# Own-token experts chosen first, and their u rows dotted during retrieval and gate building, in a conv/DeltaNet/PEER block

## What is computed

```python
def peer(h, w_q, sub_keys, u_tab, v_tab):
    q = (h @ w_q).reshape(B, T, PEER_HEADS, 2, PEER_HALF)        # 8 heads, 2 halves of 128
    s = jnp.einsum('bthpd,hpnd->bthpn', q, sub_keys)             # 128 keys per half
    v1, i1 = lax.top_k(s[..., 0, :], K)                          # K = 16
    v2, i2 = lax.top_k(s[..., 1, :], K)
    cand = (v1[..., :, None] + v2[..., None, :]).reshape(B, T, PEER_HEADS, K * K)
    cidx = (i1[..., :, None] * PEER_NKEYS + i2[..., None, :]).reshape(B, T, PEER_HEADS, K * K)
    top_s, pos = lax.top_k(cand, K)
    eidx = jnp.take_along_axis(cidx, pos, axis=-1)
    gates = jax.nn.softmax(top_s, axis=-1)
    ...  # per token, its 8 * 16 = 128 experts
        act = jax.nn.gelu(jnp.einsum('btd,bted->bte', hb, jnp.take(u_tab, ib, axis=0)))
        return jnp.einsum('bte,bted->btd', gb * act, jnp.take(v_tab, ib, axis=0))
```

## Time and profile before

| | us |
|---|---|
| median of 3 runs | 2196.34 |
| the profiled execution, its own time | 2198.44 |
| its span, first to last instruction | 2196.6 |
| TensorE busy in the span | 1880.5 |
| VectorE busy | 1477.7 |
| ScalarE busy | 729.6 |
| GpSimd busy | 709.8 |

### The profile page before, as it was taken

One profiled execution on the slowest core, in us unless ns is written; L12 is line 12 of the kernel. 1 busy time (PEld: TensorE's weight loads), 2 busy tenths in 40 slices (PEclk: granted clock), 3 DMA queues, 4 the chain that ended last, 5 costly groups with the idle time before them and its releaser, 6 DMA issues. The chain is left out here.

```text
span 2196.6 us, 33505 instructions
## 1 busy us (share of the span) xinstructions
PE 1880.5 (86%) x11429; PEld 1645.8 (75%) x11429; DVE 1477.7 (67%) x2682; ACT 729.6 (33%) x1060; POOL 709.8 (32%) x435
## 2 busy tenths in 40 slices
PE   2997678879986999968885998998998989989897
PEld 1765467768875999958874777787887878878797
DVE  5999544542313999999992667765766767768664
ACT  3235322233315444423432323332323323233233
POOL 1443111214442455521113222233443444435310
PEclk8999877779998999978997999999999998999999
DMA  7751000012222343324556888888888888788861
GB/s 298 261 180 48 1 2 0 0 38 94 97 77 77 132 136 131 123 76 169 191 205 245 310 294 297 295 284 307 279 265 296 275 305 279 263 311 283 296 212 57
DMA packets 160491, 411.22 MB, mean 187 GB/s; under 512 B 13496, under 2 KB 76088, under 8 KB 158784
## 3 DMA queue, kind: packets, MB, share of 16 engines
q1 hardware_dynamic: 115520, 264.13, 34.1%
q0 software_dynamic: 36864, 134.23, 18.6%
q10 hardware_dynamic: 8064, 12.32, 1.5%
HBM read 373.15 MB, written 37.49 MB: 187 GB/s over the span
## 5 line engine op out<-in xcount | busy, mean ns | idle before, releaser
L1645 PE MATMUL bank<-v_hi,coef_hi 128*128 128x512 f32 x768 | 305.0, 397 | 44.1 <-DVE coef_lo L1737 44.1
L1645 PE MATMUL bank<-v_hi,coef_lo 128*128 128x512 f32 x768 | 305.0, 397 | 0.0
L1645 PE MATMUL bank<-v_lo,coef_hi 128*128 128x512 f32 x768 | 304.9, 397 | 0.0
L1635 PE MATMUL bank<-h_hi,u_hi 128*128 128x384 f32 x608 | 220.1, 362 | 67.1 <-ACT gelu L1697 65.8
L1624 POOL DMA_INDIRECT own_rows<-in_u_rows_dram,own_row x128 | 154.8, 1209 | 349.6 <-DVE own_rows L1744 200.6
L1624 POOL DMA_INDIRECT own_rows<-in_peer_v_dram,own_row x128 | 189.8, 1483 | 230.4 <-DVE y_own L1801 217.4
L1635 PE MATMUL bank<-h_lo,u_hi 128*128 128x384 f32 x608 | 216.7, 356 | 0.0
L1635 PE MATMUL bank<-h_hi,u_lo 128*128 128x384 f32 x608 | 216.1, 355 | 0.0
L1737 DVE TENSOR_TENSOR v_lo<-v_tile,v_hi 128x1024 fp32r<-128x1024 f32 x128 | 156.2, 1220 | 76.5 <-ACT v_hi L1680 76.3
L1737 DVE TENSOR_TENSOR u_lo<-u_tile,u_hi 128x1024 fp32r<-128x1024 f32 x76 | 92.8, 1221 | 170.5 <-ACT u_hi L1674 170.5
L1645 PEld LDWEIGHTS bank<-v_hi,coef_hi 128*128 128x128 f32 x768 | 147.1, 192 | 78.0 <-issue 49.1
(11 more groups left out here) (326 smaller groups left out, 4106.2 us busy)
## 6 DMA issues: line engine op xcount, KB each, us to landing
v_tile<-in_peer_v_dram SPq DMA_DIRECT2D x128, 512.0 KB, 9.4
u_tile<-in_peer_u_dram SPq DMA_DIRECT2D x76, 512.0 KB
ada<-in_w_ada_dram SPq DMA_DIRECT2D x48, 512.0 KB, 4.9
gate_scratch<-gate_block SPq DMA_DIRECT2D x12, 2048.0 KB, 7.3
gate_tiles<-gate_scratch SPq DMA_DIRECT2D x32, 768.0 KB
piece<-in_peer_u_dram SPq DMA_DIRECT2D x36, 512.0 KB, 3.3
merge_w<-in_w_merge_dram SPq DMA_DIRECT2D x32, 512.0 KB, 3.3
wring<-in_w_proj_dram SPq DMA_DIRECT2D x28, 512.0 KB, 5.4
```

What stands on the lines that cost most here:

```text
L1635: last = nc.tensor.matmul(bank[b][:, 0:TD], w[:, b, k, :], x[:, k, 0:TD], start=(k == 0 and n == 0), stop=(k == KT - 1 and n == 2))
L1645: last = nc.tensor.matmul(y_bank(t, half)[:], w[:, j, t * P:(t + 1) * P], x[:, j, c], start=(first and n == 0), stop=(final and n == 2))
```

## The change

1. The candidates for a head's top 16 are cut from 256 sums to 80: those of the first rank of half one with all 16 of half two, ranks 2 to 8 with the first 8, and ranks 9 to 16 with the first. Decoding a position into two ranks takes five more small operations.
2. Retrieval is written in another order and without loops on all engines but VectorE. All 16 w_q products come first. Behind each head's second half the own tile's scores are formed, and VectorE runs the top 16 of the own tile alone, 8 heads, then lists its rows, and takes its softmax and `h_own`. Then VectorE loops over the 8 heads again for the three dense tiles, with eight own dots spread through each (`fill`), and TensorE multiplies eight u tiles per head. u tiles in retrieval: 2 + 64 + 2 = 68.
3. GpSimd fetches own rows between its subtractions, in order: one fetch, which waits for the dot four rows back, then one subtraction.
4. Gate building has six u tiles in each iteration (behind units 0, 1, 2, 4, 5 and 6) and none behind the loop: 36. Their subtraction moves to VectorE, and VectorE does one own dot behind each unit. GpSimd only fetches. Before the last iteration SyncE loads the first four v tiles and activations of the expert stage, whose buffers are now allocated ahead.
5. In the expert stage 104 expert tiles are early and 24 late. 16 own u rows and 128 v rows remain: none behind an early group's first expert and one behind the others, two or three behind a late one, to the end of the stage. Behind an early expert `coef_lo` now comes ahead of the own operation. ScalarE, VectorE and SyncE are written without loops.

```diff
-U_HEAD, U_TAIL, S_TAIL = 4, 4, 4
-N_RETR = PH * U_HEAD + U_TAIL
-N_EARLY = N_RETR + TD // TB + S_TAIL
+R = 4
+G = 4
+U_HEAD, U_MID, U_TAIL, U_UNITS = 8, 2, 2, (0, 1, 2, 4, 5, 6)
+U_ITER = len(U_UNITS)
+NR = TD // (2 * TB)
+N_RETR = U_MID + PH * U_HEAD + U_TAIL
+N_EARLY = N_RETR + NR * U_ITER
+DOT_HEAD, DOT_ITER = 8, 8
+U_DONE = PH * DOT_HEAD + NR * DOT_ITER
+OWN_GELU = 5 * G
+def own_rows_of(e):
+    i, j = e // G, e % G
+    if i == 4:
+        return 1
+    if i == 5:
+        return 0
+    if e < N_EARLY:
+        return int(j > 0)
+    return 3 if j < 3 else 2 + (i < N_EARLY // G + 2)
...
+            def fetch(pool, n):
+                if n >= R:
+                    pool.wait_ge(row_used, n - R + 1)
+                pool.indirect_dma_start(own_rows[:, n % R], None, tables[n // NS],
...
 retrieve_stage, tensor
-                with pe.Fori(0, PH) as h:
-                    for p in range(2):
-                        product(h, p, bank[p][:])
+                for h in range(PH):
+                    for p in range(2):
+                        if h:
+                            pe.wait_ge(q_ready, 2 * h - 1 + p)
+                        product(2 * h + p, bank[p][:], T)
+                        if p == 0 and h:
+                            own_scores(h - 1)
...
+                for h in range(PH):
+                    for m in range(U_HEAD):
+                        early(B0 + h * U_HEAD + m)
+                        if m == U_HEAD // 2 - 1 and h + 1 < PH:
+                            scores(h + 1)
 retrieve_stage, gpsimd
-                with pool.Fori(0, (PH * NP + U_TAIL) // 2) as i:
-                    for n in range(2):
-                        rest(n, i * 2 + (n + 1))
+                for n in range(B0 + 2):
+                    rest(n)
+                pool.wait_ge(*VO.after("own_row"))
+                for n in range(R):
+                    fetch(pool, n)
+                n = R
+                for m in range(PH * U_HEAD):
+                    while n - R < (m + 1) * DOT_HEAD // U_HEAD:
+                        fetch(pool, n)
+                        n += 1
+                    if B0 + 2 + m < NPIECE:
+                        rest(B0 + 2 + m)
 retrieve_stage, vector
+                with dve.Fori(0, PH) as h:
+                    topk(VA, h, OWN, lambda i: None)
...
+                with dve.Fori(0, PH) as h:
+                    def dot(i):
+                        n = h * DOT_HEAD + i
+                        dve.wait_ge(row_landed[i % R], h * (16 * DOT_HEAD // R) + (16 * (i // R) + 16))
+                        nc.vector.scalar_tensor_tensor(rows[:, i % R], rows[:, i % R], 1.0, h_own[:], ALU.mult, ALU.mult,
+                                                       accum_out=own_act[:, bass.ds(n, 1)]).then_inc(row_used, 1)
+                    topk(VB, h, DENSE, dot)
 scatter_stage, vector, behind a unit
+                        if u in tile_of:
+                            m = tile_of[u]
+                            dve.wait_ge(hi_ready, i * U_ITER + (m + 1))
+                            nc.vector.tensor_tensor(w_lo[:, m % 2], w[:, m % 2], w_hi[:, m % 2].bitcast(F32), ALU.subtract).then_inc(lo_ready, 1)
+                        for d in range(u * DOT_ITER // NU, (u + 1) * DOT_ITER // NU):
+                            n = i * DOT_ITER + (PH * DOT_HEAD + d)
 scatter_stage, sync
+                for j in range(G):
+                    sp.dma_start(vt[:, j], a["peer_v"][j]).then_inc(s_v[j], 16)
+                    sp.dma_start(gel_x[:, j], acts[j]).then_inc(s_act[j], 16)
+                body(NR - 1, False)
 expert_stage, vector, behind the coefficients
+                    for r in range(k):
+                        if r == min(1, k - 1):
+                            dve.wait_ge(c_hi_ready, e + 1)
+                            rest(c_lo[:, j], coef[:, e % 2], c_hi[:, j]).then_inc(c_lo_ready, 1)
+                        own(n)
+                        n += 1
```

## The result

The changed kernel takes 2158.45 us, the kernel before 2194.53 (medians of 4 runs each): ratio 0.9844, 95% interval 0.9801 to 0.9888. The forecast was 2199, no change. The time lies inside the range of 2134 to 2246, but outside the 2175 to 2225 of the case that I held likeliest (0.38): the change makes the kernel 1.6% faster.

The account below looks back on a forecast made before the run. Bounds before: TensorE in retrieval, VectorE in gate building, transfers in the expert stage until 2087. Expert loads from 1441 (+259), stage 747 (-256), tail 11.6: 2199.6 span, +1.8 -2.1 gives 2199 us; range 2134 to 2246.

Parts of the forecast that it names:

- the case that I held likeliest: Whole kernel: the forecast itself, 2199 us with its own range of 2175 to 2225; chance 0.38.
- 29.5 + 12.8: Retrieval, per dense head: 29.5 us of VectorE's own work plus 12.8 lost to eight GpSimd subtractions, 1.6 each.
- the 1.5 that I had charged for waits on VectorE's own results: Retrieval, per head: 1.5 us of waits within VectorE's own work, part of the 19.4 before dots.
- the announced 1.9: Retrieval: sign of the forecast, own dots with a mean of about 1.9 us, well over 1.22.
- Rival 1: Retrieval: VectorE and GpSimd fit beside each other, TensorE bounds at 34.9 us per head; -59, 2140 us; chance 0.24.
- Rival 2: Expert stage: early groups shorten to 17.5 us as own rows go and the landing falls; -45, 2154 us; chance 0.13.
- the preload: Gate building: expert-stage loads ahead of the last iteration's u loads cost 4 us more.
- Rival 3: Gate building: GpSimd's fetches delay VectorE's gated_i operations, 48 x 0.8 = 38 us, giving 2237; chance 0.25.
- the rule from the Trainium skill: Gate building: VectorE instructions in a 2-port mode and any GpSimd instruction exclude each other, so VectorE would wait for fetches.
- 0.7 off the landing: Expert stage, early groups: one row fewer beside v's landing makes it 0.7 us shorter.
- the change-over: Expert stage: 6 us added to the late groups' sum of 241 us for the change-over.
- the chain gate wait, landing, VectorE: Expert stage, early groups: VectorE's chain 10.6, SyncE's issue 0.8, landing 8.5 less 0.7, 0.3 between; together 19.3 us.

## Why the prediction was wrong

Of the 41.4 us of span that the forecast was too high, 22.7 arose ahead of the expert stage and 19.2 in it.

**Retrieval, the step that failed.** I had a head at 42.3 us, "29.5 + 12.8". Measured: 38.0, from these two rows of the kernel after, VectorE's start of the second dense head and its first operation behind the eighth:

```profile
856.68 0.67 DVE L1397 MAX8 top_half<-scores 128x8 f32<-128x128 f32 x3
...
1122.73 1.93 DVE L1492 TENSOR_TENSOR gates<-top_all 128x384 f32<-128x384 f32 x1
```

The mechanism was right: VectorE is busy 298 of 309 us of the loop, and operations are stretched beside GpSimd. One dot (1.21 when alone), and two small operations of the same form and shape, of which the second meets a subtraction that starts at 879.94:

```profile
861.55 2.71 POOL L1368 TENSOR_TENSOR piece_lo<-piece,piece_hi 128x1024 fp32r<-128x1024 f32 x1
...
862.74 2.60 DVE L1511 SCALAR_TENSOR_TENSOR own_rows<-own_rows,h_own 128x1024 f32<-128x1024 f32 x1
```

```profile
879.78 0.19 DVE L1439 TENSOR_SCALAR top_ab<-top_at 128x48 uint32<-128x48 uint32 x1
879.88 2.53 DVE L1440 TENSOR_SCALAR top_ab<-top_at 128x48 uint32<-128x48 uint32 x1
```

Both terms were mis-sized. Own work is 26.9, not 29.5. Where the 2.6 lie is an estimate: dots take 1.14 each from start to start, where I had 1.26, which is 1.0; and the 1.5 that I had charged for waits on VectorE's own results hardly show, as dots stand there. Stretching is 11.1, not 12.8, and of other operations than I had thought: dots are only 3.6 of it (64 x 0.45 / 8), the two rank_hot operations 4.0, the cast 1.8, and five small ones on 128x48 elements 1.7. Seven heads of 38.0 instead of 42.3 are 30 us. The first head took 43.3, not 48: 5 more. The dense loop started at 813.4, not 806, and from its end to gate building it was 12.4, not 8: 12 back. Sum: 23. Dots at 1.66 us instead of the announced 1.9 showed it; so did TensorE's waits, 2.4 us a head instead of 7.4. Rival 1 (products bound, 34.9) had neither its mechanism nor its floor: the floor is 35.6. Rival 2 gave 2154, 4 us from the measured time, but that is luck: it wanted early groups of 17.5, and they kept 19.2.

**Gate building** held. 271 us for six iterations and the preload, as forecast, though by two errors that offset each other: most iterations took 43.9 instead of 44.5, and the preload cost 9.3 instead of 4. Rival 3, fetches that hold up gated_i, is refuted by rows: it keeps 2.14 us with a fetch beside it, and every other whole group of eight that meets a fetch takes 2.13 to 2.17.

```profile
1187.67 1.68 POOL L180 DMA_INDIRECT own_rows<-in_u_rows_dram,own_row  x1 [3.79 <-DVE own_rows L1579]
...
1188.45 2.14 DVE L1570 TENSOR_SCALAR gated_i<-cst,idxT,gateT 128x128 f32<-128x128 f32 x8
```

That also answers the rule from the Trainium skill, SBUF — State Buffer, § Who interferes with whom, which I had weighed: its case of any GpSimd instruction did not show for these tensor_scalar operations and the fetch, though the same operations are held up by a subtraction.

**Early groups** held: 19.2 against 19.3, a landing of 7.9 on average against 7.8, a chain of 10.7 against 10.6. But I had taken 0.7 off the landing for the row that is gone, and that is not shown: with `coef_lo` back in its old place the row is gone as well, and the landing is 8.9, beside 9.0 in the kernel before and 8.0 in it with 80 candidates. The 9 us by which TensorE's early part was shorter (489.9 against 499) are the first groups, whose v tiles were there, and groups with fewer rows.

**Late groups** came out shorter: 37.9 against 39.6, which over five is 8.5 us, and some 2 less for the change-over: 231 against 241. How much of that is an error of the forecast is open. The same stage has late groups of 38.6 to 39.0 in three other profiles, and 235 to 236 us for the six. The code without loops, which I had costed at nothing, is worth 9 to 11 us in the kernel before, but no run shows it in the groups. The place of `coef_lo` can't be the cause, since it did not change in late groups.

**What bounds the kernel** I read half right. I named the chain gate wait, landing, VectorE, and summed it right, but called the stage paced by transfers because the DMA engines were busy 0.87 of the time. They carry 321 to 365 GB/s in early groups when nothing holds SyncE's queue. The gate load's wait, at the head of the queue that v loads share, was the bound: a late group lost 39.3 - 33.2 = 6.1 us to it, an early one 19.2 - 16.3 = 2.9, so 13 groups turned from late to early save 13 x 3.2 = 42 us. That covers the change's whole gain of 38 us of span, and with the gate load moved in both kernels no gain is left that the ratios show.

## What to carry to other kernels

Where a period is a sum of waits on one queue, move the load that waits behind those that don't, before moving work between stages; here that one line gave 6% in the kernel before, where the large change gave 1.6%. A high DMA share does not show that transfers bound: compare the rate with the best that any stretch reaches, and look for what keeps the queue from issuing. Read a loop's period as a mean over its passes, for each engine by its own rows, since one engine can fall behind another. Count an operation that stands between others by the distance from its start to the next one's start. And before explaining a difference in a stage, look at how much that stage differs between profiles whose edits don't touch it.

## What the runs showed of the hardware

- TensorE's idle time went together with a lower clock: in the expert stage the granted clock rose from 0.96 and 0.95 to 0.99 and 1.00 when 64.2 us of idle time went, and 30.5 of the 94.7 us gained were shorter busy time.
- Beside GpSimd subtractions some of VectorE's single-input operations were stretched too: a 128x48 tensor_scalar from 0.19 to 2.53 us, a 128x96 cast from 0.20 to 1.95 on average. Others were not: a 128x768 tensor_reduce has a mean of 0.94 us with the subtractions on GpSimd and without. Beside fetches by GpSimd neither dots (1.21) nor gated_i (2.13 to 2.17 for eight) were.
- Gate building, with the same code, ran at about 42 or about 44 us per iteration from one kernel to another, and changed from one to the other within one execution (43.9 to 42.4 in the kernel after).
- A high share of busy DMA engines (0.81 and 0.87 in the early stretches) was no limit: with the wait in the middle of SyncE's queue gone, the same stretch moved 321 GB/s instead of 269 in the changed kernel, and 365 instead of 303 in the kernel before.
